# A two-layer hybrid encoder on one core: joint hi/lo products for the gated expert tiles, filter spectra in another order, and a second norm cut into halves

## What is computed

```
for l in range(2):
    h = rmsnorm(x, norm1_g[l]);  p = h @ w_in[l]
    a = attention(p[..., :768])                       # 8 heads, 2 key/value heads
    kf = hyena_filter_spectra(...)                    # small MLP -> 256 taps per channel -> their spectra
    y = hyena_group(p[..., 768:1536], kf, ...)        # long convolutions by the spectra
    f = fourier_group(p[..., 1536:])
    x = x + concat(rmsnorm(a), rmsnorm(y), rmsnorm(f)) @ w_out[l]
    x = x + peer(rmsnorm(x, norm2_g[l]), ...)         # the second norm, then 16384 experts
return rmsnorm(x, final_g)

def peer(x, w_query, sub_keys, u_tab, v_tab):         # product-key retrieval of single-neuron experts
    q = x @ w_query;  s = q . sub_keys;  16 best of 256 candidates per head -> idx, softmax g
    a = gelu(u_tab[idx] . x)
    return sum(g * a * v_tab[idx])
```

## Time and profile before

| | |
|---|---|
| median of 3 runs | 1910.89 us (1910.63 to 1911.23) |
| the profiled execution | 1910.28 us, its span 1908.5 us |
| PE busy | 1868.9 us, 98% of the span |
| DVE busy | 1352.4 us, 71% |
| ACT busy | 1108.1 us, 58% |
| POOL busy | 722.4 us, 38% |
| DMA | mean 168 GB/s |
| mean granted TensorE clock | 0.997 of full speed |

### The profile page before, as it was taken

How to read it: one execution, slowest core, us unless ns; L and a number is a source line. 1 busy time by engine, 2 the same in 40 slices (tenths; PEclk the granted TensorE clock), 3 DMA queues, 4 the chain that set the end, 5 groups by cost and what they waited for, 6 DMA issues and landing times.

```text
span 1908.5 us, 42015 instructions
## 1 busy us (share of the span) xinstructions
PE 1868.9 (98%) x12878; PEld 1696.6 (89%) x12878; DVE 1352.4 (71%) x2922; ACT 1108.1 (58%) x2160; POOL 722.4 (38%) x554
## 2 busy tenths in 40 slices
PE   7999999999999999999999999999999999999998
PEld 5879999999998888878888899999999988888886
DVE  5864997777777666676657559967777776666665
ACT  4744555666655555555566445556666555555555
POOL 5541786777750000010063529867777300000000
PEclk9999999999999999999999999999999999999999
DMA  5335455444445566555552445554444455555554
GB/s 201 106 116 168 157 183 179 153 143 143 145 151 186 189 227 219 189 175 187 195 147 78 145 154 186 178 177 145 147 147 144 154 188 192 192 195 190 197 188 153
DMA packets 90501, 320.07 MB, mean 168 GB/s; under 512 B 10304, under 2 KB 11072, under 8 KB 90176
## 3 DMA queue, kind: packets, MB, share of 16 engines
q1 hardware_dynamic: 90432, 319.20, 49.3%
HBM read 318.11 MB, written 1.05 MB: 167 GB/s over the span
## 4 chain that ended last, share of the span: by engine, by line
PE 92%; DVE 5%; ACT 2%; issue 1%; POOL 0%; DMA 0%; DVEq 0%; POOLq 0%; SPq 0%; ACTq 0%
PE ps L995 12%; PE ps L997 12%; PE ps L998 12%; PE ps L909 12%; PE ps L910 11%; PE ps L911 11%; PE ps L944 5%; PE ps L922 3%; PE ps L880 2%; PE ps L882 2%; PE ps L883 2%; PE ps L924 2%; PE ps L894 1%; ACT work L1141 1%; PE ps L703 1%
## 5 line engine op out<-in xcount | busy, mean ns | idle before, releaser
L1475 POOL TENSOR_TENSOR tab_lo<-raw,tab_hi 128x512 fp32r<-128x512 f32 x416 | 538.1, 1297 | 263.1 <-ACT tab_hi L1267 164.8
L2030 DVE TENSOR_TENSOR tab_lo<-raw,tab_hi 128x512 fp32r<-128x512 f32 x512 | 355.3, 695 | 256.1 <-ACT tab_hi L1373 254.1
L909 PE MATMUL ps<-x_hl,tab_hi 128*128 128x256 f32 x1792 | 517.3, 289 | 0.0
L910 PE MATMUL ps<-x_hl,tab_hi 128*128 128x256 f32 x1792 | 506.4, 283 | 0.0
L911 PE MATMUL ps<-x_hl,tab_lo 128*128 128x256 f32 x1792 | 505.9, 282 | 0.0
L1267 ACT ACTIVATE tab_hi<-raw 128x512 fp32r<-128x512 f32 x504 | 316.7, 630 | 305.4 <-PE ps L911 274.8
L995 PE MATMUL ps<-tab_lo,w_hi 128*128 128x512 f32 x1024 | 399.6, 390 | 1.1 <-DVE w_lo L2072 1.1
L998 PE MATMUL ps<-tab_hi,w_lo 128*128 128x512 f32 x1024 | 398.4, 389 | 0.0
L997 PE MATMUL ps<-tab_hi,w_hi 128*128 128x512 f32 x1024 | 398.4, 389 | 0.0
L1373 ACT ACTIVATE tab_hi<-raw 128x512 fp32r<-128x512 f32 x512 | 319.5, 624 | 97.5 <-PE ps L998 96.6
L910 PEld LDWEIGHTS ps<-x_hl,tab_hi 128*128 128x128 f32 x1792 | 342.8, 191 | 0.0
(11 more groups left out here) (232 smaller groups left out, 2621.9 us busy)
## 6 DMA issues: line engine op xcount, KB each, us to landing
raw<-tab_u SPq DMA_DIRECT2D x256, 512.0 KB, 3.2
raw<-tab_v SPq DMA_DIRECT2D x256, 512.0 KB, 3.2
raw<-w_proj SPq DMA_DIRECT2D x64, 512.0 KB, 3.5
raw<-w_proj SPq DMA_DIRECT2D x16, 384.0 KB, 3.1
work<-cdft SPq DMA_DIRECT2D x8, 256.0 KB, 5.8
work<-sub_keys SPq DMA_DIRECT2D x2, 1024.0 KB, 5.5
work<-pmat SPq DMA_DIRECT2D x4, 304.0 KB, 4.9
x<-x_in SPq DMA_DIRECT2D x2, 512.0 KB, 3.8
```

The source lines that it names most:

```text
L909: mm(bank, hi, x_lo[:, 4 * h + k, :], start=(h + k == 0), stop=False)
L910: mm(bank, hi, x_hi[:, 4 * h + k, :], start=False, stop=False)
L1475: tt(half(tab_lo, s, h), half(raw, s, h), half(tab_hi, s, h).bitcast(F32), ALU.subtract).then_inc(lo_pool.sem, 1)
L2030: v.tensor_tensor(half(tab_lo, s, h), half(raw, s, h), half(tab_hi, s, h).bitcast(F32), ALU.subtract).then_inc(lo_dve.sem, 1)
```

## The change

Three edits. (1) Tiles 48 to 127 all use `u_tile_joint` (before: 112 to 127), tile s into bank s. The addition of the halves is no longer a reduction by DVE: ACT copies the second halves of a pair of tiles to `sums` in SBUF (`keep_part`), DVE adds the first halves from PSUM (`sum_pair`), ACT takes the gelu back to PSUM, and DVE multiplies it in as before. (2) In layer 0 the four spectra start each on its own sum or difference, the Fourier group's matrix comes first and the norm last, ACT splits the first tile of `channels` ahead of the copies of the spectra, and PE's waits for the copies stand inside `channels`. (3) In the second norm x is added, squared and averaged in halves of 512 columns, block 0 ahead of the split of tile Q0. In both norms the transposes of block k and k + 4 share a bank, and PE starts its first products on the hi part alone.

The diff, cut to its core:

```diff
+        sums = sb("sums", [P, 2, 2, SEQ])
-        sums = onef[:, 0:4 * SEQ].rearrange("p (b k t) -> p b k t", b=2, k=2)
@@ PE: transpose_x, channels, qkv, head of layer 0
-                        for k in range(DT):
-                            last = tr(ps[:, first + k // 2, (k % 2) * 256 + b * P:(k % 2) * 256 + (b + 1) * P],
+                        for k in (0, 4, 1, 5, 2, 6, 3, 7):
+                            last = tr(ps[:, first + k % 4, (k // 4) * 256 + b * P:(k // 4) * 256 + (b + 1) * P],
...
+                            if k == 0 and c in (2, 4):
+                                pe.wait_ge(*at(part_done, l, 2 + c // 2))
+                            if k == 0 and c == 6:
+                                pe.wait_ge(*at(f_mean, l, 1))
...
-                    pe.wait_ge(*at(h_lo, l, k + 1))
+                    if k:
+                        pe.wait_ge(*at(h_lo, l, k + 1))
...
+                            if k == 0 and h == 0 and b == 0:
+                                pe.wait_ge(*at(h_lo, l, 1))
                             last = mm(bank, x_lo[:, k, tok], hi, start=False, stop=(k == DT - 1))
...
-                    pe.wait_ge(*at(sumdif_done, l, 1))
-                    filter_spectrum(0, 0)
-                    filter_spectrum(1, 3)
-                    fnet_matrix(l, 1)
-                    filter_spectrum(2, 2)
-                    pe.wait_ge(*at(part_done, l, 1))
-                    filter_norm(l, 0)
-                    pe.wait_ge(*at(fn_m_done, l, 1))
-                    filter_spectrum(3, 1)
-                    pe.wait_ge(*at(f_mean, l, 1))
+                    pe.wait_ge(*at(filt_done, l, TB))
+                    fnet_matrix(l, 0)
+                    for n, bank in enumerate((3, 2, 1)):
+                        pe.wait_ge(*at(sumdif_done, l, n + 1))
+                        filter_spectrum(n, bank)
+                    pe.wait_ge(*at(sumdif_done, l, 4))
+                    pe.wait_ge(*at(part_done, l, 2))
+                    filter_spectrum(3, 2)
+                    filter_norm(l, 3)
...
-                pe.wait_ge(*at(part_done, l, 4))
                 pe.wait_ge(*at(fn_m_done, l, 1))
@@ PE: second norm, gate stage
-                keep_clock(16, 1)
+                keep_clock(14, 1)
                 transpose_x(2, 4)
+                keep_clock(3, 1)
...
-                        if s % 2 == 0:
-                            pe.wait_ge(*(at(gelu_done, l, i * 2 + s // 2 - 1) if first
-                                         else at(gated, l, i * 2 + s // 2 - 1 - GATE0 // 2)))
-                        u_tile(i, s, lo_pool, LO_G)
+                        if first and s < 2:
+                            pe.wait_ge(*at(gelu_done, l, i * 2 + s - 1))
+                        elif not first and s % 2 == 0:
+                            pe.wait_ge(*at(gated, l, i * 2 + s // 2 - 1 - GATE0 // 2))
+                        u_tile_joint(i, s, lo_pool, LO_G)
                         gates(i, s, first)
@@ ACT
-                def transposed_upper(gain, ready, first):
+                def transposed_upper(gain, done, first):
                     for k in range(DT):
-                        if k % 2 == 0:
-                            act.wait_ge(*at(xT_ready, l, ready + k // 2 + 1))
+                        if k < 4:
+                            act.wait_ge(*at(xT_ready, l, done // 2 + k + 1))
+                        else:
+                            act.wait_ge(*at(h_lo, l, done + k - 3))
...
-                def gelu_in_place(n, bank):
+                def keep_part(n, bank):
                     act.wait_ge(*at(half_used, l, n * 4 + 2 * U0 + 4))
-                    fn(ps[:, bank, :], ps[:, bank, :], ACT.Gelu).then_inc(gelu_done.sem, 1)
+                    fn(sums[:, bank // 2, :, :], ps[:, bank:bank + 2, 256:512], ACT.Copy).then_inc(part_kept.sem, 1)
...
                 def gate_quad(i):
                     distances(i, 0, False)
+                    gelu_of_sums(i * 2 - 2, 0)
                     u_upper(i, 0)
                     one_hot_i(i, 0, False)
                     u_upper(i, 1)
-                    gelu_in_place(i * 2 - 1, 1)
+                    keep_part(i * 2 - 1, 2)
                     distances(i, 2, False)
+                    gelu_of_sums(i * 2 - 1, 2)
                     u_upper(i, 2)
                     one_hot_i(i, 2, False)
                     u_upper(i, 3)
-                    gelu_in_place(i * 2, 0)
+                    keep_part(i * 2, 0)
@@ POOL: layer 0
+                if l == 0:
+                    pool.wait_ge(*at(sumdif_done, l, 4))
@@ DVE
-                    dve.wait_ge(*at(half_used, l, n * 4 + 2 * U0 + 4))
-                    v.tensor_reduce(sums[:, bank // 2, :, :],
-                                    ps[:, bank:bank + 2, :].rearrange("p k (a t) -> p k t a", a=2),
-                                    AX.X, ALU.add).then_inc(summed.sem, 1)
+                    dve.wait_ge(*at(part_kept, l, n - GATE0 // 2 + 1))
+                    both = sums[:, bank // 2, :, :]
+                    v.tensor_tensor(both, ps[:, bank:bank + 2, 0:256], both, ALU.add).then_inc(summed.sem, 1)
```

169 lines of the change are left out of this document (93 added, 76 removed).

## The result

The changed kernel takes **1897.9 us** (median of 4 runs, 1896.84 to 1898.21), beside 1910.76 for the kernel before on the same chip: a ratio of 0.9932, 95% interval 0.9916 to 0.9948. The prediction was 1897.1.

The account below looks back on a forecast made before the run. PE was taken to bound the kernel, holding 92% of the chain of waits. Gate stage 5.3, layer 0's head 5.3 and second norms 3.2 summed to 13.8 us, giving 1897.1 us, range 1893 to 1902.

Parts of the forecast that it names:

- 0.042: Gate stage: PE's saving in us for each joint tile, over 128 tiles 5.3 us, bounds 3.8 to 6.4.
- the lateness of 0.06: Gate stage: DVE reaches `weigh_group` 0.06 us late in every second tile and makes it up one tile later.
- The limit of the rival, S = 1.19: Gate stage, rival of chance 0.05: if `sum_pair` costs S = 1.19 us, PE's waits use up the whole 13.8 us.
- S - 0.97: Gate stage, same rival: PE's wait in each of 64 pairs if `sum_pair` costs S us instead of 0.60.
- predicted 3.2: Head of layer 0: the part of the 3.6 us from removed waits before `channels` that is not the 0.4.
- the 0.4 for the first lo part: Head of layer 0: PE starts on the hi part of x, winning 0.4 of a 0.50 us wait.
- the clock (1.7): Head of layer 0: without the 2.77 us wait, the granted clock does not fall behind it, winning 1.7 us.
- 3.7 instead of 5.3: Head of layer 0: its whole predicted gain, 5.3 us, from 3.6 for waits and 1.7 for the clock; bounds 2.5 to 5.5.
- 1.6 a layer: Second norm: additions, squares and first product come sooner, 1.6 us a layer, 3.2 together; bounds 1.0 and 1.9 a layer.
- up to 0.3: Second norm: last squares to scaling of block 1 stays 1.29 us or shortens by up to 0.3, without scaling beside POOL's root.
- I count nothing (0 to 0.5): Head of layer 1: `qkv` starts up to 0.5 us earlier, but no gain is counted in the sum.
- POOL's lo halves pace it afterwards: Head of layer 1: reason for counting nothing, POOL's lo halves set the pace after `qkv` starts.

Follow-up runs that it names:

- experiment 1: Kernel before with only the joint tiles 48 to 111 added (ACT's copy, DVE's addition and the tail's chain included): 1905.22 us beside 1910.34.
- Experiment 2: Kernel before with only layer 0's new order of spectra, matrix, norm of the taps and ACT's copies: 1905.47 us, ratio 0.9976.
- Experiment 10: Changed kernel with DVE's scaling of block 0 in the second norm put back behind the mean of block 1, beside POOL's root: 1897.89 us.
- experiment 4: Changed kernel with layer 1's four additions of the spectra on DVE moved behind the queries' turn, as in layer 0: 1894.01 us.
- Experiment 3: Kernel before with only the changes to both norms added: 1907.06 us, ratio 0.9984.
- 6: Changed kernel with six instead of four additions in layer 1's head, put ahead of the last two lo parts of x: 1898.37 us.
- experiment 5: Changed kernel with two more additions, to an unused area, ahead of the four of the spectra in layer 1's head: 1899.76 us.
- experiment 7: Changed kernel measured once more, unaltered: 1896.74 us (1896.12 to 1898.74).
- experiment 8: Changed kernel with DVE's addition of the halves made twice for each pair of tiles: 1904.21 us, ratio 0.9966.

## Why the prediction was right, and where it was not

The 1897.1 lies 0.8 from the 1897.9 measured, and part of that closeness is luck: layer 0's head and layer 1's head gave less than predicted, the second norms more.

**Gate stage and tail: right, slightly too large.** 0.0335 a tile instead of 0.042, 4.24 us instead of 5.3, inside its bounds of 3.8 to 6.4. The 0.042 was read from rows given to 0.01; over 61 tiles the same view gives four digits. The 0.99 us at the first v tiles came from the same part and was not counted; no term of the sum stood for it. Together 5.2, and 5.1 by experiment 1.

**DVE's part: right in place, wrong in its limit.** DVE's wait is gone in one tile of two and is 0.77 in the next, as predicted; the lateness of 0.06 is smaller, 0.02 at most beside the kernel before. The limit of the rival, S = 1.19 with PE waiting S - 0.97 in each pair, was wrong: at S = 1.20 PE waits in one pair of two and the change is still 6 us faster than before. I had carried each pair's lateness as if both pairs were alike and nothing were made up. At 1.80 DVE's whole time for a pair decides, and the change is slower than the kernel before, but at about half the cost that S - 0.97 a pair gives.

**Head of layer 0: the wait and the clock right, two small terms wrong.** Experiment 2 gives 3.2 us for the waits (predicted 3.2 besides the 0.4 for the first lo part) and 1.14 for the clock (1.7). The 0.4 for starting on the hi part is not shown: up to the taps the traces of one kernel differ by more than that (1.19 and 0.56 for the changed one). And 0.63 came back as a wait ahead of the second part of the scores. So this head gives 3.7 instead of 5.3: 0.4 not shown, 0.56 less for the clock and 0.63 that came back.

**Second norm: 2.45 instead of 1.6 a layer.** The mechanism was right and each hop a little under-sized. One piece is the one that the prediction gave "up to 0.3": the root of block 1 no longer beside DVE's scaling. Experiment 10 measures it, 0.46.

**The sum.** 5.2 + 3.7 + 4.9 is 13.8, the predicted sum with its parts off by -0.1, -1.6 and +1.7. Layer 1's head takes 0.8 to 2.4 of it.

**Head of layer 1: the step that failed.** The prediction says "I count nothing (0 to 0.5)", because "POOL's lo halves pace it afterwards". It measured -2.38 in the profiled execution, -0.8 without a fall of the clock. Both halves of the step failed. PE began `qkv` 1.04 earlier, not up to 0.5, and experiment 4 shows that POOL doesn't pace the stretch, for there the gain is kept. What ate it is POOL's long instruction. DVE's lo parts of x now wait for one instruction of ACT instead of two, so they end about 0.35 sooner against POOL's lo half (the additions begin 0.06 behind it instead of 0.42), and DVE's additions and POOL's lo half meet. Experiment 3 shows that this part of the change brings it, experiment 4 that moving the additions takes it away; 6 shows that the length of POOL's instruction goes by DVE's last addition. The prediction had named the earlier start of DVE and then asked only what PE would win by it, not whom DVE would now run into. That the wait on single instructions in `transposed_lower` is the cause, and not another line of the norms' part, is argued from the starts (POOL begins 5.0 behind the start of the transposes in both kernels, DVE's additions 5.43 before and 5.06 after); it was not tried alone.

The Trainium skill (SBUF — State Buffer, Who interferes with whom) states that a VectorE instruction with two SBUF inputs contends with a GpSimd instruction that reads SBUF, and that the port pair they share is an exclusive lock. The turns of 1.5 in experiment 5 agree. A lock for one instruction at a time would make POOL wait for one addition, 0.6; the runs show that it waits for the whole row, 2.4.

What is left is the clock in the middle of both layers. Near 106 us the changed kernel had a fall of 3.41 us, the same kernel in experiment 7 one of 6.83, and experiment 8, the same up to that place, none. Near 1045 the first had 6.83 and the second 3.41, where the kernel before had 3.41: the line of -0.38. What decides it stays open. It may make up part of the spread of 2.6 us in experiment 7; single times have no trace to show it.

## What to carry to other kernels

When an edit lets an engine start earlier, follow that engine too, not only the one that is waited for: list what it does next and who else is working then, above all DVE instructions on SBUF operands beside POOL's. Put a row of such additions where POOL is idle or its result isn't awaited; it cost 1.9 to 3.4 us in one place and nothing in another. Read a per-tile saving from the first and the last of many tiles, and split a sum that came out right into its milestones before believing it.

## What the hardware showed that was not expected

POOL's instruction does not get in between DVE's additions that follow each other at 0.60: it waited for four (3.41 us instead of 1.01) and for six (3.82, though it began 0.73 behind the first). If POOL goes first, the two take turns, and each takes 1.4 to 1.5. With starts 0.06 to 0.07 us apart, six of eight traces went one way and two the other. The DVE instructions that read one operand from PSUM did not hold POOL in the one place looked at. Timeline of POOL in the changed kernel, two lo halves, of which the second ran while DVE made lo parts of x from PSUM (from 962.75):

```profile
961.52 1.97 POOL L1438 TENSOR_TENSOR tab_lo<-raw,tab_hi 128x384 fp32r<-128x384 f32 x2 [1.53 <-DVE work L1554]
```

The two took 1.97, no longer than anywhere else.
